# Layer 0's attention: the low halves of token tiles 2 to 8 shared between GpSimd and VectorE

## What is computed

```
q, k, v, xb, gb = jnp.split(h @ p['w_in'], HYB_SPLITS, axis=-1)
q = rms_norm(q.reshape(B, L, A_HEADS, HEAD_DIM), p['q_gain'])
k = rms_norm(k.reshape(B, L, A_KV_HEADS, HEAD_DIM), p['k_gain'])
v = v.reshape(B, L, A_KV_HEADS, HEAD_DIM)
...
q = apply_axial_rope(q, *rope)
k = apply_axial_rope(k, *rope)
```

## Time and profile before

| | us |
|---|---|
| median of 3 runs | 3421.89 (3421.48 to 3423.62) |
| profiled execution: span of the instructions | 3419.5 |
| TensorE busy (matmuls) | 3177.1 (93%) |
| VectorE busy | 2256.5 (66%) |
| ScalarE busy | 1874.9 (55%) |
| GpSimd busy | 626.3 (18%) |
| all 52 low halves of L1395 (both layers) | 63.6 (1.22 each) |

### The profile page before, as it was taken

How to read it: one execution, slowest core, us unless ns; L and a number is a source line. 1 busy time by engine, 2 the same in 40 slices (tenths; PEclk the granted TensorE clock), 3 DMA queues, 4 the chain that set the end, 5 groups by cost and what they waited for, 6 DMA issues and landing times. The chain is left out here.

```text
span 3419.5 us, 55558 instructions
## 1 busy us (share of the span) xinstructions
PE 3177.1 (93%) x20138; PEld 2458.6 (72%) x20138; DVE 2256.5 (66%) x2851; ACT 1874.9 (55%) x2659; POOL 626.3 (18%) x482
## 2 busy tenths in 40 slices
PE   6988989998999999998899999999897999999999
PEld 4767777784667676765788888888885676776766
DVE  4667676546666666665677676867746666666666
ACT  3545746523565666664466483755723556665654
POOL 1211010000222332221201111011100123322231
PEclk9989999997999999999999999999997999999999
DMA  6230000238888888886010100100145688888885
GB/s 224 86 127 20 1 22 1 85 132 333 305 298 289 301 286 292 287 300 196 24 41 8 41 1 8 41 7 22 41 145 203 241 289 300 285 295 283 304 287 160
DMA packets 214171, 565.37 MB, mean 165 GB/s; under 512 B 33699, under 2 KB 71272, under 8 KB 213736
## 3 DMA queue, kind: packets, MB, share of 16 engines
q1 hardware_dynamic: 203614, 529.21, 43.2%
q0 software_dynamic: 9472, 33.57, 4.3%
q10 hardware_dynamic: 906, 0.23, 0.0%
HBM read 524.00 MB, written 38.94 MB: 165 GB/s over the span
## 5 line engine op out<-in xcount | busy, mean ns | idle before, releaser
L1976 DVE TENSOR_TENSOR moe_lo<-moe_raw,moeg_hi 128x2048 fp32r<-128x2048 f32 x384 | 880.4, 2327 | 322.9 <-PE psum L2344 154.9
L1973 ACT CAST moeg_hi<-moe_raw 128x2048 fp32r<-128x2048 f32 x384 | 728.9, 1910 | 413.3 <-PE psum L2362 291.6
L1042 PE MATMUL psum<-attn_w_hi,attn_hs 128*128 128x256 f32 (+2 forms) x1440 | 376.5, 346 | 27.0 <-PEq L2640 12.4
L1519 DVE TENSOR_REDUCE attn_neg_max<-psum 128x1 f32<-128x1280 f32 (+1 forms) x216 | 292.3, 1355 | 86.7 <-PE psum L1147 86.4
L1307 ACT ACTIVATE attn_e<-psum,attn_neg_max 128x1280 f32<-128x1280 f32 (+1 forms) x216 | 265.4, 1229 | 77.6 <-DVE attn_neg_max L1519 59.3
L1147 PE MATMUL psum<-attn_ks,attn_qst 128*128 128x512 f32 (+2 forms) x1200 | 284.2, 370 | 17.2 <-ACT attn_qst L1244 6.5
L1042 PEld LDWEIGHTS psum<-attn_w_hi,attn_hs 128*128 128x128 f32 x1440 | 256.7, 192 | 58.5 <-issue 19.6
L2362 PE MATMUL psum<-moeg_hi,moeh_x_hi 128*128 128x512 f32 x960 | 265.2, 398 | 4.8 <-issue 4.8
L2362 PE MATMUL psum<-moe_lo,moeh_x_hi 128*128 128x512 f32 x960 | 262.6, 395 | 0.0
L2362 PE MATMUL psum<-moeg_hi,moeh_x_lo 128*128 128x512 f32 x960 | 261.1, 393 | 0.0
L1147 PEld LDWEIGHTS psum<-attn_ks,attn_qst 128*128 128x128 f32 x1200 | 211.4, 191 | 63.7 <-issue 12.3
(11 more groups left out here) (345 smaller groups left out, 5433.4 us busy)
## 6 DMA issues: line engine op xcount, KB each, us to landing
moe_raw<-in_l_w_gate SPq DMA_DIRECT2D x256, 512.0 KB, 4.0
moe_raw<-in_l_w_up SPq DMA_DIRECT2D x256, 512.0 KB, 5.2
moe_raw<-in_l_w_down SPq DMA_DIRECT2D x128, 1024.0 KB, 6.2
ada_w<-in_l_ada_w SPq DMA_DIRECT2D x23, 1024.0 KB, 13.7
ada1h_w<-in_l_ada_w SPq DMA_DIRECT2D x9, 1024.0 KB, 10.8
lru_ada<-in_l_ada_w SPq DMA_DIRECT2D x8, 1024.0 KB, 6.5
lru_late<-in_l_ada_w SPq DMA_DIRECT2D x8, 1024.0 KB, 11.5
out_w<-in_l_w_out SPq DMA_DIRECT2D x16, 512.0 KB, 5.3
```

The source lines that it names most:

```text
L1042: last = pe.matmul(out, hs[t % 2][:, part, k, :], right, start=(i == 0 and n == 0), stop=(i == KB - 1 and n == 2))
L1519: dve.tensor_reduce(neg_max[:, n:n + 1], m.psum[:, score_at(n):score_at(n) + hi - lo], AX.X, ALU.max, negate=True).then_inc(s["maxed"], 1)
L1973: act.copy(mm.hi[slot % 4][:, :, :], mm.raw[slot][:, :, :]).then_inc(mm.s["hi_ready"], 1)
L1976: dve.tensor_tensor(mm.lo[slot][:, :, :], mm.raw[slot][:, :, :], mm.hi[slot % 4][:, :, :].bitcast(F32), ALU.subtract).then_inc(mm.s["lo_re ...
```

## The change

In layer 0, the low half of tiles 2 to 8 is made in two parts. GpSimd makes blocks 0 to 5 (128x768), and VectorE blocks 6 and 7 (128x256); `POOL_KB = (6, 0)[l]` holds the number of GpSimd's blocks. Tiles 0 and 1 stay with VectorE, and in layer 1 nothing changes. GpSimd counts up a semaphore of its own, `h_pool`, and TensorE waits for it as well as for `h_split` before the product of such a tile (`wait_split`, 7 in each group). On GpSimd's queue the part of tile 2 stands ahead of the first `pow` of the group, and the part of tile `t + 2` behind the `pow` of tile `t` (for `t` from 1 to 6). VectorE's instruction stays at its place in the order. No DMA is added, removed or moved.

```diff
--- before.py
+++ after.py
@@ -893,11 +893,12 @@
 
     names = ("cache_loaded", "table_ready", "w_used", "z_done", "v_done",
              "squared", "ssq", "rstd", "z_read", "v_copied", "k_split", "turned", "turn_read", "q_split", "scored",
-             "maxed", "expd", "mixed", "pv_done", "o_read", "o_squared", "o_rstd", "o_normed", "k_stored", "k_new")
+             "maxed", "expd", "mixed", "pv_done", "o_read", "o_squared", "o_rstd", "o_normed", "k_stored", "k_new", "h_pool")
     s = {n: sem(f"a{l}_" + n) for n in names}
     s["w_loaded"], s["tables_loaded"] = pre.w_loaded, pre.tables_loaded
     s["h_high"], s["h_split"], s["w_high"], s["w_split"] = pre.h_high, pre.h_split, pre.w_high, pre.w_split
 
+    POOL_KB = (6, 0)[l]
     turns_k = KT + 1
     TURNS = turns_k + 2 * NT + 3 * (units - per_tile) + per_tile + (0, 2)[l]
     nvalues = (units // 2, units)[l]
@@ -1019,9 +1020,19 @@
         @block.gpsimd
         def _(pool):
             with pool.Fori(0, groups) as j:
+                def split_tokens(t):
+
+                    wait_value(m, pool, s["h_high"], j * NT + (t + 1))
+                    pool.tensor_tensor(hs[t % 2][:, 1, 0:POOL_KB, :], h[:, 0:POOL_KB, t * P:(t + 1) * P],
+                                       hs[t % 2][:, 0, 0:POOL_KB, :].bitcast(F32), ALU.subtract).then_inc(s["h_pool"], 1)
+
+                if l == 0:
+                    split_tokens(2)
                 for t in range(NT):
                     wait_value(m, pool, s["ssq"], j * NT + (t + 1))
                     pool.tensor_tensor(m.rstd[:, 0:nz], m.ssq[:, 0:nz], m.neg_half[:, 0:nz], ALU.pow).then_inc(s["rstd"], 1)
+                    if l == 0 and 1 <= t and t + 2 < NT:
+                        split_tokens(t + 2)
                 if l == 1:
                     for u in range(units):
                         wait_value(m, pool, s["o_squared"], j * units + (u + 1))
@@ -1032,6 +1043,11 @@
 
         @block.tensor
         def _(pe):
+            def wait_split(j, t):
+                pe.wait_ge(s["h_split"], j * NT + (t + 1))
+                if l == 0 and t >= 2:
+                    pe.wait_ge(s["h_pool"], j * (NT - 2) + (t - 1))
+
             def products(j, t, out, lo, hi):
 
                 for i, k in enumerate(w_order if t == 0 else range(KB)):
@@ -1044,7 +1060,7 @@
                 return last
 
             def project(j, t):
-                pe.wait_ge(s["h_split"], j * NT + (t + 1))
+                wait_split(j, t)
                 if t == 0 and not (isinstance(j, int) and j == 0):
                     pe.wait_ge(s["expd"], j * nmaps)
                 if t >= 2:
@@ -1097,7 +1113,7 @@
                         turn_keys(i)
 
                 def last_z():
-                    pe.wait_ge(s["h_split"], j * NT + NT)
+                    wait_split(j, NT - 1)
                     at = next_bank(last=("zv", "z")[l])
                     products(j, NT - 1, m.psum[:, at:at + zw], 0, zw).then_inc(s["z_done"], 1)
                     if l == 0:
@@ -1391,9 +1407,10 @@
 
             def split_tokens(j, t):
 
+                first = POOL_KB if t >= 2 else 0
                 dve.wait_ge(s["h_high"], j * NT + (t + 1))
-                dve.tensor_tensor(hs[t % 2][:, 1, :, :], h[:, :, t * P:(t + 1) * P],
-                                  hs[t % 2][:, 0, :, :].bitcast(F32), ALU.subtract).then_inc(s["h_split"], 1)
+                dve.tensor_tensor(hs[t % 2][:, 1, first:KB, :], h[:, first:KB, t * P:(t + 1) * P],
+                                  hs[t % 2][:, 0, first:KB, :].bitcast(F32), ALU.subtract).then_inc(s["h_split"], 1)
 
             def split_weights(j, ks_):
                 for k in ks_:
```

## The result

| | before | after |
|---|---|---|
| median of 20 runs, us | 3420.49 (3412.67 to 3425.99) | 3426.23 (3416.98 to 3429.96) |
| ratio, 95% interval | | 1.002 (1.0013 to 1.0026) |
| profiled span, us | 3419.5 | 3426.7 |
| VectorE busy, us | 2256.5 | 2265.3 |
| GpSimd busy, us | 626.3 | 654.8 |

The changed kernel is 5.7 us slower (4.4 to 8.9 by the interval). It was forecast to be 3.8 slower, at 3425.7.

What follows compares the result with a forecast made beforehand. VectorE's 4.67 us a tile was taken to bound layer 0's projections, ahead of TensorE's 4.30. With the exclusion, +1.3 and +2.5 us in the two groups gave +3.8 on a median of 3421.89: 3425.7, range 3416.8 to 3430.

Steps and rivals of the forecast that it cites:

- What bounds the kernel: Layer 0's projections: a chain alternating between VectorE, 4.67 us a tile, and TensorE, 4.30 us.
- The recurrence: Six trace times chained from c(2), giving ScalarE's square of each tile 3 to 8 in a group.
- VectorE's and GpSimd's shares: Fourteen low halves drop from 1.23 to 0.42 us on VectorE; GpSimd's fourteen subtractions take 1.83 us each.
- The exclusion: VectorE and GpSimd wait for each other's SBUF instructions; GpSimd's subtraction makes VectorE's multiplication by rstd 1.45 us late.
- c - b: Time from VectorE's reduction of tile t to its low half for tile t+2: from 3.53 to 4.98 us.
- The group's start: Tile 2's subtraction queued ahead of the first pow: c(2) 0.04 us later in group 1, 1.25 late in group 2.
- c(2): Start of VectorE's low half for tile 2: 254.53 before, forecast at 254.57 in group 1.
- Sum: Last tile's square later by 1.3 us in group 1 and 2.5 in group 2: +3.8 us in all.
- The first (side by side): Rival: no exclusion, or a hidden one, between VectorE and GpSimd; -4.8 us, 3417.1, chance 0.15.
- The second (the clock): Rival: TensorE's granted clock falls inside the projection loop; +12 us, 3434, chance 0.10.
- the likeliest case: Exclusion as worked out in layer 0's projections: 3425.7 us, own range 3423 to 3429, chance 0.70.

Runs made afterwards that it cites:

- the relief: Kernel before with VectorE's low half of tiles 2 to 8 cut to blocks 6 and 7, nothing on GpSimd: 3416.27 us, ratio 0.9981.
- the subtraction without the relief: Changed kernel, but VectorE makes all 8 blocks and GpSimd's subtraction goes to places nobody reads: 3437.18 us, ratio 1.0038.
- the fills: Changed kernel with GpSimd's subtraction replaced by two fills of the same 128x768: 3418.62 us, ratio 0.9992.
- the repeated run: Changed kernel measured and profiled again with no edit: 3425.99 us, ratio 1.0014, loops 39.57 and 40.74 us.
- 2 blocks: Changed kernel with GpSimd's share cut from 6 blocks to 2 and VectorE's raised to 6: 3421.68 us, ratio 1.0.
- the new orders: Kernel before with VectorE's low half ahead of the multiplication by rstd; variants also transpose keys one tile later, then scale on GpSimd: 3415.52, 3414.43, 3414.45, 3412.30 us.

## Why the prediction was right, point by point

*What bounds the kernel.* Right. The recurrence gave a loop of 34.7 us for the relief without a hold (288.5 - 253.84); 34.70 were measured. TensorE's wait is one for VectorE's cycle.

*VectorE's and GpSimd's shares.* L1412 took 0.42 (0.42 taken), GpSimd's subtraction about 1.9 with its short waits (1.83 taken), TensorE starts at 260.31, c + 0.48 (0.47). What it waits for just ahead of that is the split keys, which the forecast did not name; in most tiles it costs nothing, as VectorE makes them right before the low half.

*The exclusion.* Right, and the step on which the sign hangs: c - b came to 5.00 (4.98), VectorE's cycle to 5.35 (5.32). It is shown from both sides, by the relief without the subtraction (-4.7 us) and by the subtraction without the relief (+15.0), and by the fills, beside which the multiplication is not held.

*The group's start.* Mis-sized for group 1. c(2) was forecast at 254.57 and came at 254.49, which looks like a hit, but by luck: tile 1 was finished 0.75 us earlier than in the profile before (253.09 for 253.84), and the start of the group could not pass that on. VectorE was held at the rotary sum, and L1474 had to wait for `pow`. Tile 2 took 6.37 us (6.11 in the repeated run) for the 5.69 of the sum. In group 2, c(2) came at 457.70, 0.5 behind the 457.17 forecast, and so did its tile 1: the start was sized right there.

*A term left out.* The transposes of the first queries stand behind those of the keys, and wait 0.38 us with them: 5.89 for 5.64 in the tile with queries. With what follows, tiles 5 to 8 together took 0.35 us more than the sum in group 1.

*Sum.* Loops of 38.7 and 40.3 us were forecast (37.40 + 1.3 and 37.82 + 2.5), and 39.6 to 39.8 and 40.7 measured at full clock: +5.1 us for the two groups in place of +3.8, the terms above. That the time came out within 0.5 us of the forecast (3426.23 for 3425.7) is partly luck: the forecast stood on a median of 3421.89 for the kernel before, which became 3420.49 with more runs, and the change cost 1.9 us more than forecast.

*The rivals.* The first (side by side) is out. The second (the clock) was given 0.10 as a case by itself; it came true as a part. In the profiles of kernels with a subtraction of 6 or 8 blocks on GpSimd (six profiles, twelve loops) the clock fell inside six loops; with the kernel before, the relief, the fills, 2 blocks and the new orders (eight profiles, sixteen loops) in none. One stretch cost 1.4 us (42.18 against 40.74), two 2.7, where 1.5 to 2.5 each was forecast. Whether such stretches make the +5.7 of the first measurement is not shown: the repeated kernel had +5.1 in its median and +5.1 in its loops at full clock, and 0.6 us is within the intervals. How often the clock falls is counted from few profiles. The range of 3416.8 to 3430.0 held the median, and the sign was that of the likeliest case.

## What to carry to other kernels

An engine with little work is not a free one if it shares its way to memory with the engine that it is to relieve. Look in the trace for a pair of instructions of both engines that overlap: if one is longer there than by itself, price the offload as time taken from the busy engine. Here 1.9 us on GpSimd took 1.5 from VectorE to spare it 0.8. The wait was cured better by the order (-7.8 us, and no work moved): what the other engine waits for goes ahead of what nobody waits for, on both sides of the hand-over.

## What the runs showed of the hardware

GpSimd's fill of 128x768 (0.74 us) held a VectorE cast of 128x64 (0.74 for 0.20) but not a multiplication of 128x256 (0.43). GpSimd's subtraction held multiplications and sums with both inputs in SBUF (1.91 for 0.42), a cast (1.70 for 0.20) and a scaling with one input, but not a multiplication with one of its two inputs in PSUM (0.55). That scaling, of 5 values, took 2.26 us at 248.90, for 0.17 by itself, while GpSimd subtracted beside it: a short instruction is held as long as a long one, until GpSimd's ends.

TensorE's granted clock fell to the lower level, for 3.4 us at a time in all but one case (6.8), in six of the twelve loops with a subtraction of 6 or 8 blocks on GpSimd, where TensorE stands still in nearly every tile, and in none of the sixteen others; I had expected it to stay. No pause of TensorE's matmuls just before a fall was longer than 2.3 us. The pause alone does not decide it: ahead of the falls of the changed kernel it was 1.76 and 1.09 us, and in the repeated execution, with 1.73 and 1.09 us at the same places, the clock stayed at 1.00. What decides it stays open.
